# A two-layer decoder trunk: a per-tile router, and eight attention heads placed among the last input projections

## The chip, the cores and the metric

The kernel runs on one core of one Trainium2 chip. The metric is the device time of one execution in microseconds (us). TensorE is called PE here (its weight loads PEld), VectorE DVE, ScalarE ACT, GpSimd POOL; SP issues most of the DMA transfers.

## What is computed

Two layers over 256 tokens of width 1024. Layer 0 is a gated MLP mixer and a dense SwiGLU; the change doesn't touch it. Layer 1 is forgetting attention (16 heads of 64) and an expert SwiGLU, top 2 of 8. Each half of a layer ends in a residual sum and a layer norm, and each layer in a gated per-layer embedding. The part that matters here:

```
def fox_mixer(x, w_in, b_f, w_out):
    q, k, v, f = jnp.split(x @ w_in, [width, 2 * width, 3 * width], axis=-1)
    log_f = jax.nn.log_sigmoid((f + b_f).astype(jnp.float32))
    c = jnp.cumsum(log_f, axis=1).transpose(0, 2, 1)
    for blk in range(s // FOX_BLOCK):
        logits = jnp.einsum("bhtd,bhsd->bhts", q[:, :, q0:q1], k[:, :, :q1])
        logits = logits + c[:, :, q0:q1, None] - c[:, :, None, :q1]
        probs = jax.nn.softmax(jnp.where(mask, logits, -jnp.inf), axis=-1)
        outs.append(jnp.einsum("bhts,bhsd->bhtd", probs, v[:, :, :q1]))
    return o @ w_out

def moe_swiglu(x, w_router, w_gate, w_up, w_down):
    top_vals, top_idx = lax.top_k((x @ w_router), TOP_K)
    weights = jax.nn.softmax(top_vals, axis=-1)
    for e in range(N_EXPERTS):
        out = out + combine[..., e:e + 1] * swiglu(x, w_gate[e], w_up[e], w_down[e])
```

## The kernel before

Everything is written out by hand: each engine has its own program, and semaphores tie them together. No scheduler reorders anything, so an engine that waits holds all that stands behind it in its program. The 256 tokens are two tiles of 128 (T = 2). Weights come in granules of 1 MB (`raw`, 6 slots). ACT rounds each granule to a high part (L604), DVE computes the low part (L921), both into `split` (3 slots), and PE makes three products for each true one (`mm3`, L1478 is the helper that issues every product): high by high, high by low, low by high. `hth` and `htl` hold the high and low parts of the transposed activations.

**Attention.** Six projections of 512 columns (N_FIN = 6, two granules each, 48 products) make q, k and v in PSUM banks 0 to 3 in turn; ACT copies each to `q_nat`, `k_nat` or `v_nat` (L779, L781; semaphore `fin_copied`). The running sums c of the log forget gates are put as two extra columns beside q and k. Then a loop of 19 steps runs the 16 heads as a pipeline. At step s PE transposes q and k of head s (L1806), makes the logits of head s-1 (`qk_t`), transposes the probabilities of head s-2 (L1827) and multiplies the transposed probabilities of head s-3 with v. DVE takes the maxima (L1255), copies the transposed probabilities out of PSUM (L1262), inverts the row sums and scales the result by them (L1269). ACT copies q and k (L795) and makes the exponentials (L802). After the loop `o_nat` is transposed by PE in 16 pieces, split into high and low part by ACT and DVE (L619, L936), and the output projection (four granules, `fox_w_out`) begins. It ends in the norm that makes h of layer 1 (L1009 to L969).

**Router.** PE multiplies h with `w_router` for both tiles (`small`, products with `wrh` and `wrl`), ACT copies the logits (L762), PE turns them (L1773), and DVE ranks them: best and second best (L1304), ties broken by `prio` (L1315 to L1320), membership (`member_b`). PE counts ranks with triangular matrices, DVE makes `slots` and the selection matrices `every` (L1297). PE then gathers each expert's tokens by products of `every` with `xh` and `xl`, the high and low part of h: ACT makes `xh` (L817), POOL makes `xl` (L557). 64 products give 16 banks of gathered tokens, which ACT and DVE copy to `xt`.

**Experts.** 56 blocks (8 experts of 7) of gate, up and down products stream 336 granules through a `ring` of 14 slots. SP loads a slot again when PE has used it, 14 granules ahead; the last two slots of the ring wait for the end of the gather. The outputs of the first seven experts go to the table `expert_rows` in DRAM and are fetched by token at the end; this holds before and after the change.

Around the attention loop PE waits for the copies and for the constants' columns:

```
        pe.wait_ge(fin_copied, T * N_FIN)
        pe.wait_ge(qk_ready, 4 * T)
        for s in range(H + 3):
```

Of the kernel before, what the change touches and what calls it, by code (L numbers as in the profile page):

```python
# [34 lines left out]
def build_trunk(nc, x, p, ln_g, ln_b, gm_w_in, gm_b_in, gm_ln_g, gm_ln_b, gm_w_s, gm_b_s, gm_w_out,  # L35
# [79 lines left out]
    o_nat, nxt = at("o_nat", [P, T, D], F32, par_a)  # L115
# [51 lines left out]
    key = route("key", [P, T])  # L167
# [56 lines left out]
    prob, nxt = at("prob", [P, 2, 3 * P], F32, nxt)  # L224
    prob_t, nxt = at("prob_t", [P, 2, 3 * P], F32, nxt)
    nmax = at("nmax", [P, 2, T], F32, nxt)[0]
    rsum = at("rsum", [P, 2, T], F32, nxt + 32)[0]
    rinv = at("rinv", [P, 2, T], F32, nxt + 64)[0]
# [69 lines left out]
    at_on = sem("at_on")  # L298
# [44 lines left out]
    def flat(t):  # L343
        return t.rearrange("p (c t) n -> p c (t n)", c=2)

# [21 lines left out]
    def _(sp):  # L367
# [57 lines left out]
        for nb in range(N_FIN):  # L425
            for half in range(2):
                load(cols(fox_w_in[0], nb * W, half))
# [50 lines left out]
    def _(pool):  # L478
# [25 lines left out]
        seq(pool.iota(iota_i[:, :], pattern=[[1, P]], base=0, channel_multiplier=0))  # L504
# [69 lines left out]
        pool.wait_ge(rows_ready, 1)  # L574
# [14 lines left out]
    def _(act):  # L589
# [136 lines left out]
        def projected(g, pp, banks):  # L726

            for i in range(2 * T):
# [30 lines left out]
        def small_out(times, bank, n):  # L759

            act.wait_ge(small_full, times)
            nc.scalar.copy(small_t[0:n, :], ps[bank][0:n, 0:S]).then_inc(small_copied, 1)  # L762
# [6 lines left out]
        for i in range(N_FIN):  # L769
            round_hi(G_FIN + 2 * i + 2)  # L770
            round_hi(G_FIN + 2 * i + 3)
            act.wait_ge(s0["used"], G_FIN + 2 * i + 2)
            what, half = i // 2, i % 2
            for m in range(T):
                bank = ps[(i + 1) % 2 * 2 + m]
# [6 lines left out]
                ins.then_inc(fin_copied, 1)  # L782
            if i == 0:
                small_out(1, 5, H)
# [3 lines left out]
            if i == 2:  # L788
                act.wait_ge(f_abs, 2)
                nc.scalar.activation(a_f[:, :, :], a_f[:, :, :], ACT.Ln).then_inc(f_log, 1)  # L790

        for s in range(H + 1):
            if s < H:
                act.wait_ge(at_qk, s + 1)
                nc.scalar.copy(qk_t[0:FA, s % 2, :], ps[6 + s % 2][0:FA, :]).then_inc(at_qkc, 1)  # L795
# [1206 lines left out]
```

## Time and profile before

| | |
|---|---|
| median of 3 runs | 1538.35 us (1537.21 to 1541.26) |
| the profiled execution | 1538.6 us, its span 1536.8 us |
| PE busy | 97% of the span |
| DVE, ACT, POOL busy | 45%, 21%, 3% |
| mean granted TensorE clock | 0.985 |
| chain that ended last | PE 93%, DVE 5% |

By time of the span: layer 0 until about 446 us, the six projections until 515 us, the attention loop and the transposes of its output until 559 us, the output projection until 582 us, norm, router and gather until 618 us, the experts until about 1497 us, then the last scatter, norm and embedding gate. Times below are us from the start of the span. A row of the timeline gives start, duration, engine, line, operation, output<-inputs, shapes and count; what stands in brackets is the idle time of the engine before it and what ended that. In the shape of a product, 128*32 is the stationary tile (rows*columns) and 128x256 what streams past it. Durations of products overlap, so the price of one is the distance from its start to the next start.

### The profile page before, as it was taken

The numbers are of one execution on the slowest core, as the hardware profiler recorded it, in microseconds if no ns is written. First come the engines' busy times: TensorE is split into PE (matmuls) and PEld (weight loads), VectorE is DVE, ScalarE is ACT, GpSimd is POOL, SyncE is SP. The second block draws the span as 40 slices with busy tenths as digits, with TensorE's granted clock in tenths as the row PEclk, the third lists the DMA queues.
The fourth block names the chain that finished last, engine by engine and source line by source line (L and its number), as shares of the span: only waits on it lengthen the run. The fifth ranks groups of instructions, "written<-read, shape, count | busy, mean of one in ns | idle before, by whom it ended". The sixth has DMA issues, their size and how long they took to land.

```text
span 1536.8 us, 33522 instructions
## 1 busy us (share of the span) xinstructions
PE 1483.4 (97%) x15041; PEld 1040.4 (68%) x15041; DVE 699.1 (45%) x1559; ACT 326.3 (21%) x461; POOL 46.5 (3%) x52
## 2 busy tenths in 40 slices
PE   7999899999899997999999999999999999999987
PEld 6888788888688886667666555555555555556665
DVE  5785665555864558332333323232323232323356
ACT  4543443433445543000000000000000000000022
POOL 2010100000100001000000000000000000000020
PEclk9999999999999998999999999999999999999998
DMA  9866455555355315899999999999999999999960
GB/s 371 301 235 211 136 172 214 188 191 191 123 179 173 109 56 192 331 393 409 408 410 406 405 409 411 409 409 406 410 405 408 402 410 404 410 407 411 403 246 28
DMA packets 196094, 468.47 MB, mean 305 GB/s; under 512 B 7740, under 2 KB 8432, under 8 KB 195440
## 3 DMA queue, kind: packets, MB, share of 16 engines
q1 hardware_dynamic: 191392, 450.92, 77.0%
q0 software_dynamic: 2992, 12.70, 2.2%
q10 hardware_dynamic: 1568, 2.75, 0.5%
q8 instruction: 115, 1.88, 0.4%
q14 instruction: 27, 0.22, 0.0%
HBM read 462.53 MB, written 3.81 MB: 303 GB/s over the span
## 4 chain that ended last, share of the span: by engine, by line
PE 93%; DVE 5%; ACT 1%; DMA 1%; issue 0%; DVEq 0%; ACTq 0%
PE ps L1478 90%; PE ps L1495 1%; DVE acc L964 1%; DVE htl L936 1%; DMA ws_raw<-in_gm_w_s_dram 0%; DVE stats L973 0%; PE ps L1806 0%; PE ps L1827 0%; PE ps L1698 0%; DVE h L969 0%; ACT hth L619 0%; DVE split L921 0%; ACT split L604 0%; DVE m_bt L1419 0%; ACT split L647 0%
## 5 line engine op out<-in xcount | busy, mean ns | idle before, releaser
L1478 PE MATMUL ps<-ring,xt 128*32 128x256 f32 (+1 forms) x8064 | 625.9, 451 | 1.1 <-DVE m_hb L1411 1.1
L1478 PEld LDWEIGHTS ps<-ring,xt 128*32 128x32 f32 x8064 | 360.5, 109 | 226.5 <-DVE m_hb L1411 1.6
L1478 PE MATMUL ps<-split,hth 128*128 128x512 f32 x1216 | 384.5, 398 | 8.7 <-DVE htl L936 4.5
L1478 PE MATMUL ps<-ring,m_bt 128*32 128x256 f32 (+1 forms) x4032 | 335.8, 451 | 0.6 <-DVE m_bt L1419 0.6
L1407 DVE TENSOR_TENSOR m_hb<-ps,m_sg 128x256 f32<-128x256 f32 x56 | 23.8, 425 | 573.1 <-ACT m_sg L863 562.7
L1478 PEld LDWEIGHTS ps<-split,hth 128*128 128x128 f32 x1216 | 230.9, 192 | 57.5 <-DVE htl L936 7.8
L1478 PEld LDWEIGHTS ps<-ring,m_bt 128*32 128x32 f32 x4032 | 183.3, 109 | 112.8 <-DVE m_bt L1419 1.0
L1419 DVE STREAM_TRANSPOSE m_bt<-m_hb 32x96 f32<-32x96 f32 x896 | 241.4, 269 | 13.1
L1478 PE MATMUL ps<-split,htl 128*128 128x512 f32 x608 | 240.0, 395 | 0.0
L863 ACT ACTIVATE m_sg<-ps 128x256 f32<-128x256 f32 x56 | 21.5, 383 | 791.7 <-PE ps L1478 791.7
L921 DVE TENSOR_TENSOR split<-raw,split 128x2048 fp32r<-128x2048 f32 x50 | 114.0, 2291 | 83.1 <-ACT split L604 83.0
L1478 PEld LDWEIGHTS ps<-split,htl 128*128 128x128 f32 x608 | 116.5, 192 | 25.1
L604 ACT CAST split<-raw 128x2048 fp32r<-128x2048 f32 x54 | 102.3, 1908 | 57.7 <-PE ps L1478 57.7
L926 DVE TENSOR_TENSOR split<-raw,split 128x2048 fp32r<-128x2048 f32 x36 | 82.0, 2291 | 34.5 <-ACT split L610 34.5
L610 ACT CAST split<-raw 128x2048 fp32r<-128x2048 f32 x36 | 68.5, 1920 | 90.9 <-PE ps L1478 90.9
L1478 PE MATMUL ps<-split,bth 128*128 128x512 f32 x224 | 69.2, 390 | 1.8 <-DVE btl L936 1.6
L1478 PEld LDWEIGHTS ps<-split,bth 128*128 128x128 f32 x224 | 41.9, 188 | 11.1 <-DVE btl L936 1.8
L1478 PE MATMUL ps<-split,btl 128*128 128x512 f32 x112 | 43.6, 389 | 0.0
L936 DVE TENSOR_TENSOR htl<-ps,hth 128x512 fp32r<-128x512 f32 x36 | 23.7, 688 | 21.8 <-ACT hth L619 21.7
L619 ACT CAST hth<-ps 128x512 fp32r<-128x512 f32 x36 | 20.3, 587 | 60.1 <-PE ps L1495 59.8
L1495 PE MATMUL ps<-ident,h 128*128 128x128 f32 x96 | 16.9, 318 | 16.7 <-DVE h L969 12.7
L1121 DVE TENSOR_TENSOR acc<-acc,ps 128x512 f32<-128x512 f32 x28 | 19.2, 686 | 28.0 <-PE ps L1478 28.0
(228 smaller groups left out, 658.3 us busy)
## 6 DMA issues: line engine op xcount, KB each, us to landing
ring<-in_moe_w_gate_dram SPq DMA_DIRECT2D x112, 1024.0 KB, 12.1
ring<-in_moe_w_up_dram SPq DMA_DIRECT2D x112, 1024.0 KB, 13.2
ring<-in_moe_w_down_dram SPq DMA_DIRECT2D x112, 1024.0 KB, 12.2
raw<-in_gm_w_in_dram SPq DMA_DIRECT2D x14, 1024.0 KB, 13.3
raw<-in_ffn_w_gate_dram SPq DMA_DIRECT2D x14, 1024.0 KB, 5.0
raw<-in_ffn_w_up_dram SPq DMA_DIRECT2D x14, 1024.0 KB, 5.9
raw<-in_ffn_w_down_dram SPq DMA_DIRECT2D x14, 1024.0 KB, 4.9
raw<-in_fox_w_in_dram SPq DMA_DIRECT2D x12, 1024.0 KB, 5.2
```

Of the source, the lines that this page charges most:

```text
L604: nc.scalar.copy(split[:, ss, 0], raw[:, slot]).then_inc(st["hi"], 1)
L610: nc.scalar.copy(split[:, gs % SPL, 0], raw[:, gs % RAW]).then_inc(s0["hi"], 1)
L619: nc.scalar.copy(dst, bank[:, 0:n].rearrange("p (c t) -> p c t", t=P)).then_inc(st["tp_hi"], 1)
L863: nc.scalar.activation(m_sg[:, 0:2 * P].rearrange("p (q n) -> p q n", n=P), ps[0][:, :].rearrange("p (q x) -> p q x", x=2 * P)[:, :, 0:P], ...
L921: nc.vector.tensor_tensor(split[:, ss, 1], raw[:, slot], split[:, ss, 0].bitcast(F32), ALU.subtract)\
L926: nc.vector.tensor_tensor(split[:, gs % SPL, 1], raw[:, gs % RAW], split[:, gs % SPL, 0].bitcast(F32), ALU.subtract).then_inc(s0["lo"], 1)
L936: nc.vector.tensor_tensor(dst, bank[:, 0:n].rearrange("p (c t) -> p c t", t=P), hi.bitcast(F32), ALU.subtract).then_inc(st["tp_lo"], 1)
L1121: nc.vector.tensor_tensor(part, part, ps[bank][:, :], ALU.add).then_inc(part_added, 1)
L1407: nc.vector.tensor_tensor(m_hb[:, 0:2 * P].rearrange("p (q n) -> p q n", n=P), ps[0][:, :].rearrange("p (q x) -> p q x", x=2 * P)[:, :, P: ...
L1419: last = nc.vector.transpose(m_bt[s * G3:(s + 1) * G3, b % 2, q, :, :], blocks[:, :, s, :])
L1478: return nc.tensor.matmul(o, a, b, start=start, stop=stop)
L1495: last = nc.tensor.transpose(ps[6 + n % 2][:, c * P:(c + 1) * P], src, ident[:, :])
```

## The change

1. **Heads among projections.** The projections come in another order of columns (`FIN_COLS`: first halves of q, k and v, then the second halves). The last three all use banks 0 and 1. The steps of attention 0 to 10 are placed among their products (`STEP_AFTER`), after every 12 products or so; steps 11 to 16 follow; steps 17 to 19 stand among the products of the output projection.
2. **Another step.** The probabilities are scaled before they are transposed (DVE, `at_norm`), one step later, and there are three `prob` buffers but only one PSUM bank for the transposes. v is now the stationary tile of 64 columns, for two heads at a time, so that the result comes out transposed in bank 5: ACT and DVE split it (`at_ohi`, `at_olo`) straight into the inputs of the output projection. `o_nat` and its 16 transposes are gone.
3. **Router.** Each tile has its own logits, turn and ranking; tile 0's products are placed ahead of tile 1's transposes. Ranking is shorter. Slots start at one instead of zero.
4. **Gather.** DVE makes `xl` (POOL no longer does), between the two halves of `every`; PE starts with the products of `xh`. The weights and the row numbers are computed after the gather's copies.

The diff, cut to its core:

```diff
-    GX_BANK = (0, 1, 4, 5, 6, 7, 0, 1, 4, 5, 6, 7, 4, 5, 6, 7)
+    GX_BANK = (6, 7, 4, 5, 0, 1, 6, 7, 4, 5, 6, 7, 4, 5, 6, 7)
+    FIN_COLS = (0, 2, 4, 1, 3, 5)
+    STEP_AFTER = {(3, 1): 0, (3, 2): 1, (3, 3): 2, (4, 0): 3, (4, 1): 4, (4, 2): 5, (4, 3): 6,
+                  (5, 0): 7, (5, 1): 8, (5, 2): 9, (5, 3): 10}
...
 POOL
-        for m in range(T):
-            pool.wait_ge(xh_ready, m + 1)
-            pool.tensor_tensor(xl[:, m, :], h[:, m, :], xh[:, m, :].bitcast(F32), ALU.subtract)\
-                .then_inc(xl_ready, 1)
+        pool.wait_ge(rows_ready, 1)
...
 ACT, after the third projection
+        for i in (4, 5):
+            round_hi(G_FIN + 2 * i + 2)
+            attend(4 * i - 13)
+            attend(4 * i - 12)
+            round_hi(G_FIN + 2 * i + 3)
+            attend(4 * i - 11)
+            fin_out(i)
+            attend(4 * i - 10)
+        for s in range(11, H + 1):
+            attend(s)
...
 DVE
+        def attend(s):
+            if 0 <= s - 2 < H:
+                hd = s - 2
+                dve.wait_ge(at_exp, T * (hd + 1))
+                seq(nc.vector.reciprocal(rinv[:, hd % 3, :], rsum[:, hd % 3, :]))
+                for m, (a, b) in enumerate(((0, P), (P, 3 * P))):
+                    part = prob[:, hd % 3, a:b]
+                    ins = nc.vector.tensor_scalar(part, part, rinv[:, hd % 3, m:m + 1], None, ALU.mult)
+                ins.then_inc(at_norm, 1)
+            if s >= 6 and s % 2 == 0:
+                p = (s - 6) // 2
+                dve.wait_ge(at_ohi, p + 1)
+                nc.vector.tensor_tensor(o_chunk(p, 1), ps[5][:, 0:S], o_chunk(p, 0).bitcast(F32), ALU.subtract)\
+                    .then_inc(at_olo, 1)
+            if 0 <= s - 1 < H:
...                (the two maxima of head s-1)
+            if 0 <= s - 3 < H:
...                (waits at_pt, copies prob_t)
...
+            seq(nc.vector.tensor_copy(lg[:, m, :], ps[3 + 2 * m][:, m * NE:(m + 1) * NE]))
             seq(nc.vector.max(top8[:, m, :], lg[:, m, :]))
+            seq(nc.vector.tensor_scalar(eqk[:, m, :], lg[:, m, :], top8[:, m, 0:1], 16.0, ALU.is_equal, ALU.mult))
...
+            seq(nc.vector.max(two8[:, m, :], eqk[:, m, :]))
+            nc.vector.tensor_scalar(member_b[:, m, :], eqk[:, m, :], two8[:, m, 1:2], None, ALU.is_ge)\
+                .then_inc(mem_ready, 1)
...
+        select_every(first_experts, (0,))
+        rest_x(0)
+        select_every(first_experts, (1,))
...
+        gathered(0)
+        route_weights()
+        rows_to_gather()
         dve.wait_ge(acc_init, 2 * T)
...
 PE
+            if s >= 5 and s % 2:
+                p = (s - 5) // 2
+                pe.wait_ge(at_ptc, 2 * p + 2)
...
+                for m in range(T):
+                    for b in range(2):
+                        hd = 2 * p + b
+                        last = mm(ps[5][b * DH:(b + 1) * DH, m * P:S], v_nat[:, m, hd * DH:(hd + 1) * DH],
+                                  prob_t[:, b, m * S:m * S + (T - m) * P], m == 0, m == T - 1)
...
+        for i in range(N_FIN):
+            if i == 2 or i == 3:
+                pe.wait_ge(fin_copied, T * (i - 1))
+            elif i > 3:
+                pe.wait_ge(fin_copied, T * i)
...
+        small(2, NE, wrh, wrl, fresh, (0,))
         turn_tile(1)
-        small(2, NE, wrh, wrl, fresh)
-        small_turn(3, NE, 2).then_inc(lg_full, 1)
+        small_turn(3, NE, 2, (0,)).then_inc(lg_full, 1)
+        pe.wait_ge(proj_copied, 3 * T)
+        small(4, NE, wrh, wrl, fresh, (1,))
+        small_turn(5, NE, 3, (1,)).then_inc(lg_full, 1)
```

PE at the end of the last projection, in the program before: the projection's last products, then step 0 of the attention loop, which waits for the copies of all projections (counting from the start of the program, lines are those of the file before).

```order
L1478 MATMUL ps<-split,hth 128x512 x2
L1478 MATMUL ps<-split,htl 128x512
L1806 MATMUL ps<-ident,q_nat 66x128 [waits qk_ready,fin_copied]
L1806 MATMUL ps<-ident,q_nat 66x128
```

In the changed program a step stands between products of the fifth projection (this is step 5, with the first pair of heads; `prob_t,v_nat` is the product with v):

```order
L1543 MATMUL ps<-split,htl 128x512
L1860 MATMUL ps<-ident,q_nat 66x128 [waits at_qkc]
L1860 MATMUL ps<-ident,q_nat 66x128
L1860 MATMUL ps<-ident,k_nat 66x128 x2
L1543 MATMUL ps<-qk_t 128x128 [waits at_exp,at_qkc]
L1543 MATMUL ps<-mask,ident_b 128x128
L1543 MATMUL ps<-qk_t 128x256
L1543 MATMUL ps<-mask,ident_b 128x128
L1543 MATMUL ps<-prob_t,v_nat 64x256 [waits at_ptc]
L1543 MATMUL ps<-prob_t,v_nat 64x256
L1543 MATMUL ps<-prob_t,v_nat 64x128 x2
L1896 MATMUL ps<-ident,prob 128x128 [waits at_ptc,at_norm]
```

What moved: steps 0 to 10 now have projection products between them, and the wait for all copies is split into smaller ones.

DVE in an even step of the changed program (here step 6): the scaling of head 4 waits for its exponentials and stands ahead of the maxima of head 5.

```order
L1264 RECIPROCAL rinv<-rsum 128x2 [waits at_exp]
L1267 TENSOR_SCALAR prob<-prob,rinv 128x128 [waits dve_step]
L1267 TENSOR_SCALAR prob<-prob,rinv 128x256
L1272 TENSOR_TENSOR otl<-ps,oth 128x256 [waits at_ohi]
L1278 TENSOR_REDUCE nmax<-ps 128x1 [waits at_log]
L1278 TENSOR_REDUCE nmax<-ps 128x1
L1285 COPY prob_t<-ps 128x384 [waits at_o,at_pt]
```

What moved: before, the maxima stood first in a step and waited for PE alone.

DVE in the router of the changed program, from the second tile's membership to the gather's copies:

```order
L1371 TENSOR_SCALAR member_b<-eqk,two_102 128x8 [waits dve_step]
L1378 TENSOR_TENSOR member<-eqk,two_102 128x16
L1379 TENSOR_TENSOR gap<-top_100 128x2 [waits dve_step]
L1383 TENSOR_TENSOR slots<-member,ps 128x2x8 [waits rank_full]
L1350 TENSOR_TENSOR every<-iota,slots 128x384 [waits dve_step]
L1350 TENSOR_TENSOR every<-iota,slots 128x384
L1357 TENSOR_TENSOR xl<-h,xh 128x1024 [waits xh_ready] x2
L1350 TENSOR_TENSOR every<-iota,slots 128x384 x2
L1433 COPY xt<-ps 128x384 [waits gx_full] x8
```

What moved: `xl` came here from POOL, and 26 small operations that stood ahead of the copies now stand behind them.

## Rows read from the trace of the kernel before

**Rows 1.** Experts: busy us by engine, then clock, DMA share, GB/s.

```profile
619.00:1500.00 881.00, 874.06 (x12105) 534.61 (x12093) 292.71 (x1025) 47.11 (x139) 13.85 (x6) 1.00 1.02 398
```

**Rows 2.** Timeline of PE: gate and up products of two expert blocks.

```profile
1251.73 9.88 PE L1478 MATMUL ps<-ring,xt 128*32 128x256 f32 x135
...
1267.27 9.88 PE L1478 MATMUL ps<-ring,xt 128*32 128x256 f32 x135
```

**Rows 3.** Timeline of ACT: copies after the third and last projection.

```profile
481.92 1.08 ACT L779 COPY k_nat<-ps 128x512 f32<-128x512 f32 x2 [3.47 <-PE ps L1478]
...
515.25 1.07 ACT L781 COPY v_nat<-ps 128x512 f32<-128x512 f32 x2 [3.48 <-PE ps L1478]
```

**Rows 4.** Timeline of PE: transposes of the output, output projection, its end.

```profile
554.76 1.97 PE L1495 MATMUL ps<-ident,o_nat 128*128 128x128 f32 x8 [0.38 <-DVE o_nat L1269]
...
558.89 1.20 PE L1478 MATMUL ps<-split,hth 128*128 128x512 f32 x2
...
582.49 1.32 PE L1495 MATMUL ps<-ident,h 128*128 128x128 f32 x8
```

**Rows 5.** Timeline of PE: start of attention, one step of it.

```profile
516.38 0.41 PE L1806 MATMUL ps<-ident,q_nat 128*66 128x128 f32 x2 [1.17 <-ACT v_nat L781]
...
520.82 0.38 PE L1806 MATMUL ps<-ident,q_nat 128*66 128x128 f32 x2
...
521.53 0.65 PE L1478 MATMUL ps<-qk_t 66*128 66x256 f32 x2
...
522.08 0.50 PE L1827 MATMUL ps<-ident,prob 128*128 128x128 f32 x3
522.41 0.78 PE L1478 MATMUL ps<-v_nat,prob_t 128*128 128x64 f32 x6
523.03 0.38 PE L1806 MATMUL ps<-ident,q_nat 128*66 128x128 f32 x2
```

**Rows 6.** Timeline of PE: router and gather.

```profile
590.75 1.32 PE L1495 MATMUL ps<-ident,h 128*128 128x128 f32 x8 [1.49 <-DVE h L969]
...
595.40 0.28 PE L1773 MATMUL ps<-ident,small_t 8*128 8x8 f32 x2 [0.45 <-ACT small_t L762]
602.77 0.22 PE L1478 MATMUL ps<-member_b,upper_b 128*128 128x8 bf16 x2 [7.09 <-DVE member_b L1324]
...
605.36 0.66 PE L1478 MATMUL ps<-every,xh 128*128 128x384 f32 x1 [2.29 <-DVE every L1297]
...
618.39 3.88 PE L1478 MATMUL ps<-ring,xt 128*32 128x512 f32 x50
```

**Rows 7.** Timeline of DVE: router.

```profile
596.42 2.32 DVE L1315 TENSOR_TENSOR eqk<-lg,top 128x16 f32<-128x16 f32 x1
598.78 2.28 DVE L1318 TENSOR_TENSOR eqk<-eqk,prio 128x16 f32<-128x16 f32 x1
...
604.18 1.96 DVE L1297 TENSOR_TENSOR every<-iota,slots 128x384 fp32r<-128x384 f32 x4
...
611.14 1.48 DVE L1367 COPY xt<-ps 128x384 f32<-128x384 f32 x3
```

**Rows 8.** Timeline of POOL: the low part of h.

```profile
596.38 4.64 POOL L557 TENSOR_TENSOR xl<-h,xh 128x1024 fp32r<-128x1024 f32 x2 [177.42 <-ACT xh L817]
```

**Rows 9.** Timeline of PE: two products of the gather, later.

```profile
614.13 0.33 PE L1478 MATMUL ps<-every,xh 128*128 128x384 f32 x1
614.31 0.33 PE L1478 MATMUL ps<-every,xl 128*128 128x384 f32 x1
```

**Rows 10.** Timeline of ACT: first and last piece of a step's exponentials.

```profile
523.00 0.37 ACT L802 ACTIVATE prob<-ps,nmax 128x128 f32<-128x128 f32 x1 [0.88 <-DVE nmax L1255]
...
523.72 0.20 ACT L802 ACTIVATION_READ_ACCUMULATOR prob<-ps,nmax 128x1 f32 x1
```

**Rows 11.** Timeline of DVE: the maxima of one attention step.

```profile
522.35 0.62 DVE L1255 TENSOR_REDUCE nmax<-ps 128x1 f32<-128x128 f32 x2 [0.70 <-PE ps L1478]
```

**Rows 12.** The same view as Rows 1, 3 us of the gather.

```profile
606.00:609.00 3.00, 3.00 (x11) 3.00 (x10) 2.56 (x15) 0.48 (x1) 0.00 (x0) 0.50 0.00 0
```

More of the change, by code:

```diff
@@ L724, in _, with projected @@
         round_hi(g + G_EXP - 1)
[L726 to L728 removed]
+        def projected(g, pp, banks, of=range(2 * T)):
+            for i in of:
                 act.wait_ge(s0["used"], g + 1)
@@ L1289, in select, with select_every @@
             ins.then_inc(sel_ready, 1)
-        def select_every(at_e):
-            for half in range(2):
+        def select_every(at_e, halves=range(2)):
+            for half in halves:
                 for m in range(T):
@@ L1754, in _, with small @@
         n_fin = nt[0] - T
-        def small(bank, n, wsh, wsl, fresh):
-            for m in range(T):
+        def small(bank, n, wsh, wsl, fresh, tiles=range(T)):
+            for m in tiles:
                 tok = slice(m * P, (m + 1) * P)
@@ new lines, in attend @@
+                mm(bank[:, 2 * P:3 * P], ident_b[:, :], mask[:, :], False, True).then_inc(at_log, 1)
+            if s >= 5 and s % 2:
+                p = (s - 5) // 2
+                pe.wait_ge(at_ptc, 2 * p + 2)
+                if p >= 1:
+                    pe.wait_ge(at_olo, p)
+                if p == H // 4:
+                    pe.wait_ge(fin_copied, T * N_FIN)
+                for m in range(T):
+                    for b in range(2):
+                        hd = 2 * p + b
+                        last = mm(ps[5][b * DH:(b + 1) * DH, m * P:S], v_nat[:, m, hd * DH:(hd + 1) * DH],
+                                  prob_t[:, b, m * S:m * S + (T - m) * P], m == 0, m == T - 1)
+                last.then_inc(at_o, 1)
@@ new lines, in out_granule @@
+        def out_granule(g, m):
+            tok = slice(m * P, (m + 1) * P)
+            for kk in range(2):
+                k = 2 * (g - G_FOUT) + kk
+                for half in range(2):
+                    last = mm3(ps[2 * m + half][:, :], oth[:, k, tok], otl[:, k, tok], g % SPL, 2 * kk + half,
+                               k == 0, False)
+            if m == T - 1:
+                last.then_inc(s0["used"], 1)
+        for i in range(N_FIN):
[3 more added lines that the diff above has]
+                pe.wait_ge(fin_copied, T * i)
+            if i < 3:
+                cols_granules(G_FIN + 2 * i, [(i + 1) % 2 * 2, (i + 1) % 2 * 2 + 1], fresh=n_fin if i == 0 else None,
+                              between={0: lambda: turn_half(1),
+                                       1: lambda: small_turn(4, H, 1).then_inc(f_full, 1)}.get(i))
+            else:
+                fin_block(i)
+            if i == 0:
+                pe.wait_ge(small_split, 4)
+                small(5, H, wfh, wfl, None)
+            if i == 2:
+                pe.wait_ge(f_logf, 1)
+                pe.wait_ge(const_ready, 1)
+                prefix(5, H, z_f, upper, ones).then_inc(c_full, 1)
```

383 lines of the change are left out of this document (203 added, 180 removed).

## The prediction

> **What bounds the kernel now.** I read the page first: PE is busy in 97% of the span, and the chain that ended last lies on PE for 93%. So only what PE does, or waits for, can move the time. The experts' stage is the longest: PE is busy 874 of 881 us in it, at the full clock [rows 1], and a block follows the last at 15.54 us (1267.27 - 1251.73) [rows 2]; 56 such blocks are 870 us. The reader is to see that this stage is a fixed length that begins when the gather ends. The change leaves its products alone. The DMA share there is as full as PE (398 GB/s), which comes back among the rivals. Everything that the change can give must come before the first expert product, at 618.39.
>
> Next I read the timeline of PE from the third projection to there, in two stretches.
>
> *Attention, 481.9 to 582.5 us, 100.6 us.* Three projections take 33.3 (from 481.92 to 515.25, the copies that follow them) [rows 3]. From 515.3 to 558.89, 43.6 us, stand the heads and the output's transposes, and from there to 582.49 the output projection, 23.6 us [rows 4]. Within the heads a step takes 2.21 us (523.03 - 520.82), back to back on PE: 1.26 for transposes of q and k and the logits, 0.33 for the transposes of the probabilities, 0.62 for the product with v [rows 5]. So PE's own work bounds the heads, 16 x 2.21 = 35.4, and the other 8.2 us are filling, emptying, the wait of 1.17 for v [rows 5] and the output's transposes with their split.
>
> *Router, 590.75 to 618.39 us.* PE waits 7.09 us for membership and 2.29 for the selection matrices; the gather takes 13.0 (605.36 to 618.39) [rows 6]. The wait of 7.09 is odd in its make-up. DVE runs two operations of 16 columns in 2.32 and 2.28 us [rows 7], while 26 operations of like size between the end of `every` (606.14) and 611.14 take 0.19 each [rows 7]. POOL's two subtractions on `xl` lie exactly beside them, 596.38 to 601.02 [rows 8]. DVE was held by POOL.
>
> **The change, part by part.**
>
> *Heads on PE.* Interleaving saves no product, so I count PE's work. Transposes and logits stay: 16 x (1.26 + 0.33) = 25.4 us. The product with v now has v as a stationary tile of 64 columns, and two heads write different halves of a bank: two products over 256 columns and two over 128. One product over 256 with its mask takes 0.55 (522.08 - 521.53) [rows 5]. One after the other the four are at most 2 x 0.55 + 2 x 0.28 = 1.65 us; two at a time, 0.83. Before, two heads cost 1.24. The experts' products of 32 columns show 135 issues of 256 columns in 9.88 us [rows 2], 0.07 each, where an issue over 256 columns of a full tile takes some 0.27 [rows 5]: narrow tiles do run side by side, four at a time. So I take the low end, with a little for switching, 0.9: 8 x 0.9 = 7.2. Heads: 32.6 us.
>
> Where the gather's full tile gives way to the experts' narrow one, the trace names no idle time ahead of the block [rows 6], and the gather's products start 0.17 apart [rows 9]. The Trainium skill (TensorEngine Tiling, Key Properties) says that changing the tiling mode drains the engine, which speaks against this step: sixteen changes. It gives no price. If each cost 0.1 us, half of them in stretches where PE waits anyway, the sum would be 0.8 us longer; the 0.9 above stays as it is.
>
> *Output's transposes.* Sixteen transposes and their splits, from 554.76 to 558.89, leave the path [rows 4]. The splits become one ACT copy and one DVE subtraction for each pair, beside PE.
>
> *Output projection.* Two issues take 1.20 us at 558.89 [rows 4], where the clock was low; without the gap before it the clock should not fall. At the projections' rate, 33.3/6 for a granule, four are 22.2; with the embedding's transposes, and a share of the 33.3 that is not granules, 22.5.
>
> *New waits.* (a) The last three projections share banks 0 and 1, so the sixth waits for the copies of the fifth. ACT has step 5's exponentials and the first output copy ahead of these copies: I find them some 1.0 us later than PE. For the fifth projection ACT is in time. (b) At the sixth's end ACT copies v (1.07 us [rows 3]) and then q and k of head 10: 0.5 us for step 11. (c) DVE now scales head s-2 ahead of the maxima of head s-1, and the scaling waits for the exponentials, which wait for the maxima. That is a loop through two engines, once a head: exponentials 0.92 (523.00 to 523.92) [rows 10], maxima 0.62 [rows 11], scaling about 0.7, the subtraction of the low part every second step 0.17, hand-overs 0.1. Sum 2.5 us, against 2.0 of PE's work. For the scaling no row exists. A reciprocal is one small operation, 0.19; the products of 128 and 256 columns cost at least 0.19 each and at most the 0.49 of 384 columns in `every` [rows 7]: 0.57 to 1.17, and I take 0.7, as one source and fewer columns are nearer the low end. Steps 0 to 10 are covered, since 12 projection products (2.8 us) lie between two steps. Steps 11 to 16 are not: 6 x 2.5 = 15.0 where PE has 12.2, so 2.8 us of waiting. If that cover didn't hold, ten more steps would lose 0.5 each.
>
> Sum: 33.3 + 32.6 + 22.5 + 1.0 + 0.5 + 2.8 = 92.7 against 100.6: **7.9 us less**. The bounds: loop at 2.3 or at 3.0, -1.2 and +3.0; pairs one after the other, about five on the path x 0.75 = +3.8; no waits, -4.3.
>
> The skill bears on the scaling alone. The one-source operations here read and write SBUF in fp32. The Trainium skill (VectorE: DVE Perf Modes, the perf-mode tier table) lets such a `tensor_scalar` run at twice the rate of a two-source operation; taken so, the scaling would be near 0.6 and the loop 2.4, and the stretch 0.6 us shorter.
>
> *Router.* POOL's hold goes: 4.6 us become 2 x 0.19, a gain of 4.2. Of the 14 operations between logits and membership, 7 are left behind the second tile's logits, tile 0's being done while that tile is still split: 7 x 0.19 = 1.3. Tile 0's 24 small products move into the 1.49 us in which PE waits for h [rows 6]; the second tile's are then held by its own split, so I count 0.5 (0 to 1.5). Slots take one operation, not four, and the count moves behind: 4 x 0.19 = 0.8 of the 2.29. Sum 6.8. What is added: `xl` on DVE, two operations of 1024 columns, at least 1.0 each and at most POOL's 2.3 [rows 8]; I take 1.2. PE meanwhile has twelve products of `xh`, 0.17 each at the full clock (614.31 - 614.13) [rows 9], 2.1 us, twice that at half. Of the 2.4 at most 0.3 shows; likely 0.1. At POOL's price it would be 2.5. The gather keeps its length: 64 x 0.175 = 11.2 at the full clock, 13.0 measured, since the clock was at half (0.50) until about 609 [rows 12], behind 7 us of idleness. There are still some 4 idle us ahead of it, so I leave that loss in. **6.7 us less.**
>
> *Behind the gather.* 29 small DVE operations (5.5 us) and an exponential on ACT now stand between the copies and the first block's hidden product. The first gate and up products cover them, 9.88 us [rows 2]. If the cover were gone, 7 us would come on top once. SP's order is as before, and POOL's next work (a memset, the table's zero row) waits for the row numbers and is needed only at the end.
>
> Total 7.9 + 6.7 = 14.6. The profiled execution took 1538.6, 0.25 over the median, so the sum gives 1524.0 against it: **1524.0 us** forecast.
>
> **The rivals.**
> - *Better cover.* The clock stays full through the router (1.8 us, 13.0 - 11.2), or the loop and the waits (a) and (b) don't show (up to 4.3). Together 1518. For it: only 4 us of idleness. Against: most of those 4 are in one piece. Chance 0.12 for under 1519.5.
> - *Pairs one after the other, or a longer loop.* +3.8 and +3.0: 1528 to 1531. For it: no product of 64 columns of this kind is in the trace. Chance 0.19 for 1528 to 1533.9.
> - *The gain is given back.* If the loads bound the experts, starting sooner would bring nothing, and the time would be 1538. For it: DMA share 1.02. Against: blocks at PE's pace of 15.54 and 7 us of idleness in 881 [rows 1, 2]; and the loads start sooner too. Chance 0.06 of within 0.3%.
> - *Slower: half clock.* In steps 11 to 16 PE idles a fifth of the time in small pieces. Should the clock fall to 1.2 GHz there and stay there over the output projection, 12.2 + 22.5 = 34.7 us of work double, less the 2.8 of waiting that this hides: +32, or 1556. It decides once more than 14.6 us of PE's work run at half. Against: a steady step before has much the same work. Chance 0.05.
>
> **How the numbers follow.** My forecast (1519.5 to 1528) has 0.58. 1516 to 1533 leaves out the last two rivals and the ends of the others, about 0.2. A measurement can tell about 0.3% (4.6 us) from no change: faster 0.89, same 0.06, slower 0.05.
>
> **What would show it.** In the profile after: no idle time of 7 us ahead of the rank products, and no DVE operation of 16 columns over 1 us; pairs of products with v at about 0.9 us; steps 11 to 16 about 2.5 us apart, with PE waiting for q, k or the copies; output projection at the full clock; the experts still 15.54 a block. The forecast is wrong if the experts' stage grows, if the clock falls in the uncovered steps, or if the router's wait moves to `xl`.

## The result, and the profile after

The changed kernel takes 1521.97 us (median; 1521.48 to 1523.24) against 1538.91 us (1537.21 to 1541.26) for the kernel before on the same chip. The ratio is 0.989, with a 95% interval of 0.9877 to 0.9903: 17 us faster, 2.0 us better than the forecast of 1524.0 and inside its range. In part that closeness is luck: terms that were off both ways partly cancel, as the section on the prediction shows. The profiled execution took 1521.48, its span 1519.7.

PE is as full as it was. First the line of the page for the engines, then the experts' stage: busy us of PE, PEld, DVE, ACT and POOL, the granted clock, the DMA share and GB/s; then two successive blocks' gate and up products on PE's timeline.

```profile
PE 1476.3 (97%) x14993; PEld 1029.4 (68%) x14993; DVE 701.8 (46%) x1581; ACT 327.4 (22%) x466; POOL 42.0 (3%) x50
```

```profile
602.00:1483.00 881.00, 874.31 (x12101) 535.10 (x12093) 297.46 (x1054) 50.55 (x143) 14.73 (x8) 1.00 1.02 398
```

```profile
1219.14 9.88 PE L1543 MATMUL ps<-ring,xt 128*32 128x256 f32 x135
...
1234.68 9.88 PE L1543 MATMUL ps<-ring,xt 128*32 128x256 f32 x135
```

They answer to [rows 1, 2]: 874 of 881 us busy, 398 GB/s, 1234.68 - 1219.14 = 15.54 us a block, as before. The gain lies ahead of the experts. Between the copies behind the third projection (481.64 after; 481.92 in [rows 3]) and the first expert product, the two stretches of the prediction are:

| stretch | before | after | gain | predicted |
|---|---|---|---|---|
| attention, to the transposes of h | 100.6 | 91.0 | 9.5 | 7.9 |
| router and gather | 35.9 | 28.7 | 7.2 | 6.7 |

With the 0.3 us by which the copies came earlier these make the 17.1 us between the spans.

**Attention.** PE's timeline in the changed kernel, from a step among the projections, through the uncovered steps 11 to 16, to the output projection and the transposes of h. Columns: start, us, then line, operation, output and inputs, shape, count, and in brackets the idle time with its releaser.

```profile
508.90 0.22 PE L1543 MATMUL ps<-mask,ident_b 128*128 128x128 bf16 x1
509.05 0.87 PE L1543 MATMUL ps<-prob_t,v_nat 128*64 128x256 f32 x8
509.85 0.55 PE L1896 MATMUL ps<-ident,prob 128*128 128x128 f32 x3
...
533.50 0.22 PE L1543 MATMUL ps<-mask,ident_b 128*128 128x128 bf16 x1
533.56 0.50 PE L1896 MATMUL ps<-ident,prob 128*128 128x128 f32 x3
533.90 0.38 PE L1860 MATMUL ps<-ident,q_nat 128*66 128x128 f32 x2
...
535.25 0.87 PE L1543 MATMUL ps<-prob_t,v_nat 128*64 128x256 f32 x8
...
539.76 0.87 PE L1543 MATMUL ps<-prob_t,v_nat 128*64 128x256 f32 x8 [0.28 <-DVE prob_t L1285]
...
542.76 0.38 PE L1860 MATMUL ps<-ident,k_nat 128*66 128x128 f32 x2
543.24 0.49 PE L1543 MATMUL ps<-qk_t 66*128 66x128 f32 x2
...
544.62 0.87 PE L1543 MATMUL ps<-prob_t,v_nat 128*64 128x256 f32 x8 [0.28 <-DVE prob_t L1285]
...
547.25 0.71 PE L1543 MATMUL ps<-split,oth 128*128 128x512 f32 x2
...
572.67 1.32 PE L1560 MATMUL ps<-ident,h 128*128 128x128 f32 x8 [0.21 <-DVE h L1006]
```

A pair of products with v lasts 0.80 us (509.05 to 509.85), with 0.15 ahead of it where a transpose comes only 0.06 behind the same product with the mask (533.50, 533.56). Steps 11 to 16 last 13.35 us (533.90 to 547.25); the reader is to see how little of it is waiting. The brackets say 0.28 twice; by the distances between starts these two pairs come 0.36 later than one that needn't wait (0.51 behind the mask product in place of 0.15). Between the transposes of k and the logits lie 0.48 us once (542.76 to 543.24), where 0.22 is usual. Leaving the narrow tile has a price too. The last issue of a pair, over 128 columns, and the first transpose behind it:

```profile
509.65 0.27 PE L1543 MATMUL ps<-prob_t,v_nat 128*64 128x128 f32 x1
509.85 0.33 PE L1896 MATMUL ps<-ident,prob 128*128 128x128 f32 x1
```

They start 0.20 apart, where issues over 128 columns within the pair follow each other at 0.11 in each half. This is part of the pair's 0.80.

What sets the pitch in these steps is on ACT and DVE: first the exponentials of three successive heads on ACT, then DVE from the first of them on.

```profile
539.27 0.37 ACT L803 ACTIVATE prob<-ps,nmax 128x128 f32<-128x128 f32 x1 [0.94 <-DVE nmax L1278]
...
541.54 0.37 ACT L803 ACTIVATE prob<-ps,nmax 128x128 f32<-128x128 f32 x1 [0.88 <-DVE nmax L1278]
...
544.13 0.37 ACT L803 ACTIVATE prob<-ps,nmax 128x128 f32<-128x128 f32 x1 [0.94 <-DVE nmax L1278]
```

```profile
540.22 0.17 DVE L1264 RECIPROCAL rinv<-rsum 128x2 f32<-128x2 f32 x1 [0.52 <-ACT prob L803]
540.42 0.55 DVE L1267 TENSOR_SCALAR prob<-prob,rinv 128x128 f32<-128x128 f32 x2
540.89 0.61 DVE L1278 TENSOR_REDUCE nmax<-ps 128x1 f32<-128x128 f32 x2
...
542.69 0.55 DVE L1267 TENSOR_SCALAR prob<-prob,rinv 128x128 f32<-128x128 f32 x2
543.15 0.42 DVE L1272 TENSOR_TENSOR htl<-ps,hth 128x256 fp32r<-128x256 f32 x1
543.48 0.61 DVE L1278 TENSOR_REDUCE nmax<-ps 128x1 f32<-128x128 f32 x2
```

The loop of the prediction is there: exponentials from 539.27, reciprocal at 540.22, scaling at 540.42, maxima at 540.89, the next exponentials at 541.54. It takes 2.27 us, and 2.59 where the low part of the output stands between scaling and maxima (543.15 to 543.48): 2.43 a head.

**Router.** PE, from the rank products to the first expert product; then DVE, in the second tile's ranking and at `xl`; then the clock in the gather's first part.

```profile
586.92 0.20 PE L1543 MATMUL ps<-member_b,upper_b 128*128 128x8 bf16 x2 [1.66 <-DVE member_b L1371]
...
588.62 3.78 PE L1543 MATMUL ps<-every,xh 128*128 128x384 f32 x12 [1.42 <-DVE every L1350]
592.23 2.24 PE L1543 MATMUL ps<-every,xl 128*128 128x384 f32 x12
...
601.34 1.93 PE L1543 MATMUL ps<-ring,xt 128*32 128x512 f32 x23
```

```profile
585.97 0.23 DVE L1367 SCALAR_TENSOR_TENSOR eqk<-lg,top,eqk 128x8 f32<-128x8 f32 x1
586.23 0.17 DVE L1369 TENSOR_TENSOR eqk<-eqk,prio 128x8 f32<-128x8 f32 x1
...
588.39 2.35 DVE L1357 TENSOR_TENSOR xl<-h,xh 128x1024 fp32r<-128x1024 f32 x2
```

```profile
588.00:592.00 4.00, 3.38 (x11) 3.41 (x12) 3.68 (x6) 0.00 (x0) 0.00 (x0) 0.57 0.47 180
```

The waits of 7.09 and 2.29 us [rows 6] are 1.66 and 1.42. No small DVE operation is longer than 0.23, where two took 2.32 and 2.28 [rows 7]. `xl` takes 2.35 on DVE for both tiles, and PE doesn't wait for it. The gather takes 12.72 us (588.62 to 601.34); the clock is at half from 588.4 to 591.8 (0.57 in the mean of the row). Before it was at half from 598.9 to 609.1, of which 3.8 us lay in the gather [rows 12], so that the gather itself lost nearly as much then.

### The profile page after: what moved, and what is told of

Read it like the earlier page. It is cut to its first block, busy times and chain, and to the rows that moved or that the text cites. A ratio compares the mean times of both kernels' runs of the same rounds, so it can differ in the third digit from the quotient of the medians.

```text
span 1519.7 us, 33431 instructions
## 1 busy us (share of the span) xinstructions
PE 1476.3 (97%) x14993; PEld 1029.4 (68%) x14993; DVE 701.8 (46%) x1581; ACT 327.4 (22%) x466; POOL 42.0 (3%) x50
## 4 chain that ended last, share of the span: by engine, by line
PE 92%; DVE 5%; ACT 1%; DMA 1%; issue 1%; DVEq 0%; ACTq 0%
PE ps L1543 90%; PE ps L1560 1%; DVE acc L1001 1%; DVE stats L1010 0%; DMA ws_raw<-in_gm_w_s_dram 0%; DVE htl L973 0%; ACT split L613 0%; PE ps L1763 0%; DVE h L1006 0%; DVE split L958 0%; PE ps L1860 0%; PE ps L1896 0%; ACT hth L628 0%; DVE m_bt L1485 0%; ACT prob L803 0%
## 5 line engine op out<-in xcount | busy, mean ns | idle before, releaser
L1543 PE MATMUL ps<-split,hth 128*128 128x512 f32 x1184 | 374.3, 398 | 8.7 <-DVE htl L973 4.5
L1543 PEld LDWEIGHTS ps<-split,hth 128*128 128x128 f32 x1184 | 223.6, 191 | 56.0 <-DVE htl L973 7.8
L1543 PE MATMUL ps<-split,htl 128*128 128x512 f32 x592 | 233.5, 394 | 0.0
L1543 PEld LDWEIGHTS ps<-split,htl 128*128 128x128 f32 x592 | 113.1, 191 | 24.3
```

The costliest lines, as they stand in the source:

```text
L1543: return nc.tensor.matmul(o, a, b, start=start, stop=stop)
```

## The experiments

Where a kernel's time is one single run, I compare stretches of its trace instead; the last section says why. The attention stretch is then measured from `z_f,upper`, the small table products behind the third projection (481.44 in the changed kernel), to the transposes of h (572.67): 91.23 us, and to the start of the output projection (547.25): 65.81.

**The parts alone.** First the router's part alone, then attention's part alone; each takes the other part's text from the kernel before. One piece of each, against the changed kernel (the loop of PE in the first, `xl` in the second):

```
-        for s in range(11, H + 1):
-            attend(s)
...
+        for s in range(H + 3):
```

```
-                rest_x(dve.snap(r * T))
...
+            pool.tensor_tensor(xl[:, m, :], h[:, m, :], xh[:, m, :].bitcast(F32), ALU.subtract)\
+                .then_inc(xl_ready, 1)
```

> The kernel before with the router and gather part of the change alone (per-tile ranking, low part of h on DVE, weights after the gather). Theory (the two parts lie one behind the other on PE's path and add up): the stretch from the first transposes of h to the first expert product shortens from 35.9 to about 28.7 us, and the kernel takes 1538.9 - 7.2 = 1531.7 us. Rival (the router's stretch got shorter only because the loads and the clock stood otherwise after the new attention): less than 4 us gained, above 1535 us.

> The kernel before with the attention part of the change alone (heads among the last projections, the new step, no transposes of the output). Theory: the stretch up to the end of the output projection shortens by 9.8 us as in the whole change, the router keeps its 35.9 us with DVE held twice for 2.3 us; about 1529.1 us. Rival (the parts help each other): the two single gains together are under 14 us.

Measured: the router alone 1532.94 us (1530.51 to 1533.76), ratio 0.9952 (0.9935 to 0.9968) to 1539.74 of before. Attention alone 1530.2 (1528.65 to 1530.54), ratio 0.9935 (0.9918 to 0.9952). The gains are 6.8 and 9.5, together 16.3, against 17; each of the two has an interval of some 2.5 us either way, so the stretches say more. In the trace of the first, transposes of h to the first expert product is 28.77 us (583.75 to 612.52), as in the changed kernel; in that of the second it is 35.71 (573.96 to 609.67), with the old waits of 7.09 and 2.29. Each part shortens its own stretch and leaves the other's as it was.

**POOL's hold.** `xl` goes back to POOL, all else stays:

```
+            pool.tensor_tensor(xl[:, m, :], h[:, m, :], xh[:, m, :].bitcast(F32), ALU.subtract)\
+                .then_inc(xl_ready, 1)
...
-        rest_x(0)
```

> The changed kernel with the low part of h made by POOL again, the rest as it is. Theory (POOL's subtractions hold DVE): they start when the high part is ready, about 586 us, in the midst of the second tile's ranking; a DVE operation of 8 or 16 columns there takes about 2.3 us in place of 0.2, once or twice, so that the first expert product comes 2 to 4.5 us later than at 601.3. Rival (the long operations of before had another cause, the wide operands or the shape of the operation): no DVE operation of the ranking over 0.3 us, first expert product within 0.7 us of 601.3, since POOL's 4.6 us would end about when the twelve products with the high part do.

Measured: 1526.66 us. DVE and POOL during the second tile's ranking, and PE at the rank products:

```profile
585.64 2.41 DVE L1371 SCALAR_TENSOR_TENSOR eqk<-lg,top,eqk 128x8 f32<-128x8 f32 x1
585.68 4.64 POOL L570 TENSOR_TENSOR xl<-h,xh 128x1024 fp32r<-128x1024 f32 x2 [167.21 <-ACT xh L858]
...
588.08 2.26 DVE L1373 TENSOR_TENSOR eqk<-eqk,prio 128x8 f32<-128x8 f32 x1
...
590.88 0.22 PE L1546 MATMUL ps<-member_b,upper_b 128*128 128x8 bf16 x2 [5.95 <-DVE member_b L1375]
```

Two operations of 8 columns take 2.41 and 2.26 us instead of 0.23 and 0.17 while POOL's two subtractions run, 4.27 in all, and PE's wait grows from 1.66 to 5.95. The stretch from the transposes of h to the first expert product is 34.11 us (572.34 to 606.45) against 28.67, 5.4 more and not the 2 to 4.5 that I expected. Of these, 4.3 are the hold and 1.1 the gather, 13.86 against 12.72, as the clock was at half from 588.0 to 598.2 here and from 588.4 to 591.8 in the changed kernel. That this 1.1 comes from the hold isn't shown: two kernels below without a hold have gathers of 14.00 and 14.10. The Trainium skill (GPSIMD Engine Reference, Specifications) says that GpSimd's SBUF interfaces are shared with VectorE and contend with its instructions that have two SBUF inputs. The trace agrees: both held operations have two.

**The maxima first.** In the changed kernel DVE scales head s-2 ahead of the maxima of head s-1. Here it is the other way round:

```
         def attend(s):
+            if 0 <= s - 1 < H:
...
             if 0 <= s - 2 < H:
...
-            if 0 <= s - 1 < H:
```

> The changed kernel with the maxima of head s-1 ahead of the scaling of head s-2 in DVE's step. Theory (steps 11 to 16 are bound by the loop exponentials, scaling, maxima): the loop is cut, two steps take PE's 4.1 to 4.3 us in place of 4.86, and the output projection starts 0.7 to 1.4 us sooner than at 547.25. Rival (they are bound by DVE's or ACT's work, or by the single bank of the transposes): steps stay at 4.86 for two.

Measured: 1524.41 us, of which 1.2 over the changed kernel's trace lie ahead of the table products and 1.3 in the gather, so that the attention stretch has to decide. The output projection starts 66.39 us behind the table products, not 65.81, and the transposes of h 91.80, not 91.23. So taking the scaling out of the loop brought nothing. PE waits more, and elsewhere:

```profile
537.08 0.87 PE L1543 MATMUL ps<-prob_t,v_nat 128*64 128x256 f32 x8 [0.57 <-DVE prob_t L1285]
...
541.86 0.87 PE L1543 MATMUL ps<-prob_t,v_nat 128*64 128x256 f32 x8 [0.57 <-DVE prob_t L1285]
```

Two steps last 4.78 us (541.86 - 537.08), against 4.86 in the changed kernel (544.62 - 539.76). But the pair now waits 0.57 for `prob_t`, already at the first uncovered pair: DVE copies the transposed probabilities behind maxima, scaling and low part, and in these two steps it waits itself, 0.71 for PE's logits and 0.25 for PE's transposes. I read this as a second loop, through PE, that has taken the first one's place; no run tests that reading. The order moved the wait and hardly changed the length of a step.

The gather of this run shows something else. Its router has the same program and the same waits, and yet it took 14.00 us (590.37 to 604.37). Its first products, and the clock from 592 to 596:

```profile
590.37 4.18 PE L1543 MATMUL ps<-every,xh 128*128 128x384 f32 x12 [1.42 <-DVE every L1350]
```

```profile
592.00:596.00 4.00, 4.00 (x14) 4.00 (x14) 1.56 (x4) 0.48 (x1) 0.00 (x0) 0.50 0.00 1
```

The clock was at half from 589.4 to 596.3. Among the seven traces with this router and without extra products or POOL's subtractions, five have gathers of 12.60 to 12.84 us (the changed kernel's 12.72 among them) and two of 14.00 and 14.10. What makes the difference stays open.

**The low part behind the maxima.** Only the subtraction, 0.33 us in every second step, goes out of the loop:

```
+            if 0 <= s - 1 < H:
...
             if s >= 6 and s % 2 == 0:
...
-            if 0 <= s - 1 < H:
```

> The changed kernel with one edit on VectorE: in the even steps the subtraction of the low part stands behind the maxima, not ahead of them. In the changed kernel the exponentials of the uncovered steps are 2.27 and 2.59 us apart in turn. Theory (the loop of exponentials, scaling and maxima sets the pitch there, and the subtraction lies in it only in even steps): both become 2.27, PE's work of 2.11 a head nearly fills it, and the output projection starts 0.6 to 0.8 us earlier (65.0 to 65.2 us behind the last small table products, against 65.81); time 0.7 below the changed kernel. Rival (VectorE's whole work in a step sets the pitch, so its order does not matter, as with the maxima first, which gave nothing): 65.7 to 65.9, no change.

Measured: 1523.25 us. Exponentials of four heads on ACT:

```profile
536.74 0.37 ACT L803 ACTIVATE prob<-ps,nmax 128x128 f32<-128x128 f32 x1 [0.37 <-DVE nmax L1273]
...
539.00 0.37 ACT L803 ACTIVATE prob<-ps,nmax 128x128 f32<-128x128 f32 x1 [0.89 <-DVE nmax L1273]
...
541.26 0.37 ACT L803 ACTIVATE prob<-ps,nmax 128x128 f32<-128x128 f32 x1 [0.61 <-DVE nmax L1273]
...
543.52 0.37 ACT L803 ACTIVATE prob<-ps,nmax 128x128 f32<-128x128 f32 x1 [0.88 <-DVE nmax L1273]
```

They are 2.26 us apart each time. The output projection starts 65.26 us behind the table products (548.97 - 483.71), 0.55 earlier, and so do the transposes of h (90.68 us behind them, not 91.23). That is what the loop, and not DVE's whole work, demands; it is somewhat under the 0.6 to 0.8 expected. The single time doesn't show it, because this run's opening was 2.3 us later.

**Without the cover.** All 17 steps stand behind the sixth projection, nothing else changes:

```
-    STEP_AFTER = {(3, 1): 0, (3, 2): 1, (3, 3): 2, (4, 0): 3, (4, 1): 4, (4, 2): 5, (4, 3): 6,
-                  (5, 0): 7, (5, 1): 8, (5, 2): 9, (5, 3): 10}
+    STEP_AFTER = {}
...
-        for s in range(11, H + 1):
+        for s in range(H + 1):
```

> The changed kernel with all steps of attention after the last projection, the projections in two pairs of banks in turn as before; the new step, its transposed output and the steps among the output projection stay. Theory (the loop through ACT and DVE costs 2.43 us a head where nothing covers it, PE's work is 2.0): the output projection starts 5 to 7 us later than 547.25, the whole takes 1527 to 1529 us, still below the attention of before since the output's transposes are gone. Rival (placing heads among projections brings nothing, as PE does the same products anyway; all the gain is from the transposes that went): within 1.5 us of 1522.

Measured: 1528.3 us (1528.08 to 1529.88), ratio 0.9925 (0.9908 to 0.9942) to before: 6.3 above the changed kernel, or 5.4 by the two ratios. The output projection starts 71.91 us behind the table products (553.96 - 482.05), 6.1 later. PE's waits from 515 to 554 (us in total, how often, the longest):

```profile
PE ps L1524 <- DVE prob_t L1274: 1.7, 6, 0.3
PE ps L1841 <- ACT v_nat L788: 1.2, 1, 1.2
PE ps L1524 <- ACT qk_t L795: 1.1, 3, 0.4
PE ps L1877 <- DVE prob_t L1274: 0.5, 2, 0.3
```

So of attention's 9.5 us, the cover gives two thirds, part of it by removing the wait for v that stood ahead of the first head (1.17 in [rows 5]) and the filling behind it. The remaining third, about 3.4, stays without the cover. I put it down to the cheaper product with v and the output's transposes that are gone, less the waits of the new loop; no run takes these apart.

**Side by side or not.** Two kernels on the pair of products with v. The first issues head by head (256 columns, 128, 256, 128) where the changed kernel issues both products of 256 columns first. The second writes both heads to the same half of the bank; the upper 64 rows of each output piece are then not computed.

```
-                for m in range(T):
-                    for b in range(2):
+                for b in range(2):
+                    for m in range(T):
```

```
-                        last = mm(ps[5][b * DH:(b + 1) * DH, m * P:S], v_nat[:, m, hd * DH:(hd + 1) * DH],
+                        last = mm(ps[5][0:DH, b * S + m * P:b * S + S], v_nat[:, m, hd * DH:(hd + 1) * DH],
```

> The changed kernel with the four products of a pair with v in the order head, then token tile, so that neighbours write the same half of the bank but for one place. Theory (products of 64 columns in different halves run side by side, and the order gives them the chance): a pair takes 1.2 to 1.5 us in place of 0.8 (the middle two may still overlap), the last projection ends 1 to 2 us later and the whole takes 1523.5 to 1526. Rival (the engine runs them one after the other in either order, and 0.8 is simply their price): no change.

> The changed kernel, but the products with v of both heads of a pair write the same 64 partitions (partitions 0 to 63) of the bank, head by head; the upper 64 rows of the attention output are then not computed, and the times are to be read so. In the changed kernel a pair takes 0.80 us in either order. Theory (the two heads' narrow products run side by side in different halves of TensorE, and the order does not matter because each half takes its own in turn): in one half they must run one after the other, the pair takes about 1.3 to 1.45 us. Then the three pairs between projections (steps 5, 7, 9) and the one in the output projection add 0.5 to 0.6 each, and the uncovered ones partly: stretch from the last small table products to the transposes of h 93 to 95 us against 91.2, time about 1524.5. Rival (they never ran side by side, a narrow product is simply cheap): the pair stays at 0.80 and the stretch at 91.2, time 1522.

Measured: head by head 1521.15 us, and the pair lasts 0.81 (508.71 to 509.52), as before: my expectation fell. Same half 1526.4 us, and the pair lasts 1.44. First PE's instructions by shape, head by head, in the window from 508.70 to 509.15 (count, then busy us and mean ns); then the timeline of the same half.

```profile
L1543 PE MATMUL ps<-prob_t,v_nat 128*64 128x256 f32 x4 | 0.7, 404 | 0.0
```

```profile
508.88 1.51 PE L1543 MATMUL ps<-prob_t,v_nat 128*64 128x256 f32 x8
510.32 0.55 PE L1896 MATMUL ps<-ident,prob 128*128 128x128 f32 x3
```

The second kernel shows that the heads do run side by side: without it a pair costs 0.64 us more, the transposes of h come 95.06 us behind the table products (576.32 - 481.26), 3.8 later. Eight pairs would be 5.1; the waits of 0.28 ahead of the uncovered pairs are gone in this run, which accounts for part of the missing 1.3. The time lies 1.9 above the expected 1524.5, of which 1.4 is this run's gather (14.10, see above). The first shows why the order is nothing: each product is two issues, and by 509.15 all four over 256 columns have started and none over 128, though the issues over 128 columns of head 0 stand between them in the program. They don't hold the other half's products. The Trainium skill (TensorE: Matmul & The Clock Gate, Part 3, The mechanism) says that matmuls start and end strictly in program order. This trace shows another order than the kernel's text for products in different halves, and the measurement decides. Whether the chip changed the order, or the instructions already came to it in this one, no run here tells.

**The gather's clock.** 26 bf16 products ahead of the rank products and 22 ahead of the gather, which nothing reads, keep PE at work during the two waits:

```
+        for _ in range(26):
+            mm(ps[6][:, 0:P], ident_b[:, :], upper_b[:, :], True, True)
         pe.wait_ge(mem_ready, T)
...
+        for _ in range(22):
+            mm(ps[6][:, 0:P], ident_b[:, :], upper_b[:, :], True, True)
         gather(0, 1, T)
```

> The changed kernel with 26 and 22 idle products of 128 columns (bf16, into a bank that the gather overwrites) on PE ahead of its waits for membership and for the selection matrices; they add work and no result. Theory (the clock at half in the first products of the gather comes from PE's idleness before it): the granted clock stays at full, the first twelve products take 2.1 us in place of 3.6, and the first expert product comes 1 to 1.5 us sooner relative to the start of the ranking. Rival (the 3.6 us are waits or the fall has another cause): the half clock and the 3.6 us stay.

Measured: 1520.85 us. PE's twelve products of `xh`, and the clock beside them:

```profile
589.34 2.33 PE L1543 MATMUL ps<-every,xh 128*128 128x384 f32 x12 [0.17 <-DVE every L1350]
```

```profile
588.00:592.00 4.00, 3.83 (x36) 3.51 (x34) 3.96 (x7) 0.55 (x2) 0.00 (x0) 1.00 0.61 231
```

The gather starts as before, 15.96 us behind the transposes of h (15.95), and its first twelve products take 2.33 instead of 3.78. It is 1.3 us shorter (28.67 to 27.36 for the stretch), and the clock is granted full. So half the clock, behind waits of 1.66 and 1.42 us with little between, is what the gather still lost: with the extra products it takes 11.40 us, without them 12.60 to 12.84 or, twice, 14.00 and 14.10.

**Both together.** The extra products with the maxima first, and with the low part behind:

> The changed kernel with both the maxima first and the idle products. Theory: the two gains add, 1.7 to 2.9 us below the changed kernel's 1522, 1519.1 to 1520.3 us. Rival (what is gained ahead of the experts is lost in the first block, as DVE's 29 small operations behind the gather then end later than the first gate and up products): no faster than 1522.

> The low part behind the maxima, and the 26 and 22 extra bf16 products ahead of the rank products and of the gather, whose results nothing reads. Theory: the two gains add, 0.7 (uncovered steps) and 1.3 (gather at the full clock), so about 1520.0 us against 1522.0 of the changed kernel. Rival: only the extra products count, 1520.7. Should either cost more than it gives: 1522 or above.

Measured: with the maxima first 1522.27 us (1521.1 to 1523.29), ratio 0.9882 (0.9865 to 0.9898); no gain beyond the changed kernel's 0.989. Its attention stretch is 0.6 longer (91.82), its gather 1.3 shorter. With the low part behind 1520.76 (1520.24 to 1521.6), ratio 0.9882 (0.9866 to 0.9899). In the trace of the latter, from the table products to the first expert product, 118.00 us (482.09 to 600.09) stand against 119.90: 1.9 less, 0.6 of it in the uncovered steps and 1.3 in the gather. The medians differ by 1.2, and the two intervals overlap, so that it is faster is shown by the stretches and not yet by the times.

## Why the prediction was right, step by step

- *The bound.* The experts' stage is a fixed length that begins when the gather ends: 15.54 us a block before and after, and no gain was given back. That rival (0.06) is out.
- *POOL's hold, ranking and small products, 6.0 us.* Measured from the transposes of h to the rank products: 20.28 before (582.49 to 602.77), 14.25 after, so 6.03. The hold itself, 4.2 in the sum, is 4.3 in the run that brings it back.
- *Slots, 0.8.* From the rank products to the gather 2.59 before, 1.70 after: 0.9.
- *`xl` on DVE, 1.2 us for each of two, nearly hidden.* Both took 2.35, against the 2.4 of the sum. They were hidden, since PE's twelve products of `xh` took 3.6 at the half clock. At the full clock, in the run with the extra products, `xl` ends at 591.46 and its first product starts at 591.52, some 0.1 us behind the twelve products of `xh`, which is the 0.1 of the sum.
- *The gather, unchanged.* It became 0.3 us shorter, where I had it 0.1 longer. I kept the whole loss to the clock although the waits ahead shrank from 9.4 to 3.1 us, and that was nearly right: 3.8 us of the gather ran at half before, 3.2 after. It is also luck, since two other traces with the same router and the same waits have 1.3 us more.
- *A pair at 0.9 us.* 0.80, and 0.95 with what lies ahead of it. Side by side is shown. The Trainium skill's (TensorEngine Tiling, Key Properties) drain at a change of mode fits the prices here, about 0.1 us going in (0.15 against 0.06) and about 0.1 coming out (0.20 against 0.11), the size that was supposed; both are small beside the 0.64 that running side by side saves.
- *Waits (a) 1.0 and (b) 0.5.* Neither is there. PE comes to step 6 right behind the fifth projection; its 1.5 us of transposes, logits and probabilities (512.99 to 514.51) hide the copies, which are 1.08 (from 513.19). I had set ACT's lateness against the next projection product and left out the step in between. The same holds for (b).
- *The loop, 2.5 us a head, 2.8 of waiting.* The pitch was right (2.43; scaling with reciprocal 0.67 for 0.7), its count was not. I charged all six steps. Step 11 and the pair at 535.25 still lived on the lead that DVE and ACT had from the covered steps, and the last head's transposes and the last two pairs stand among the output projection's products, where nobody waits for them. Of 13.35 us about 1.4 is waiting, by the distances between starts: 0.36 ahead of each of two pairs, 0.34 ahead of the last transposes (0.40 in place of 0.06), and for q and k 0.26 ahead of the logits and 0.11 within them.
- *PE's own work.* Here I was about 1.3 too low: a head's share without waits is 2.08 (535.25 to 539.76 are 4.51, less 0.36, halved), not 2.04, which is 0.6 over sixteen heads; the rest, about 0.7, falls to the output projection. So 2.9 too much waiting and 1.3 too little work make the 1.6 by which attention came out better. The total was closer than its terms.
- *Cover gone, 0.5 a step for ten steps.* 6.1 us in the stretch, not 5: the filling of the pipeline and the wait for v, which I hadn't put into that figure, are covered as well.
- *The slower rival, half clock from step 11 on.* The clock was 1.00 through the attention stretch; the half clock that before fell at the output's transposes (0.57 over 554 to 562) isn't there.

## What to carry to other kernels

When a loop through two other engines is slower than the main engine's work, charge its lag only to the steps that have neither a lead behind them nor other work among them; here the pitch was right and the count was not. Ahead of moving an operation to the front of such a loop, look for the next loop: here taking the scaling out moved the wait, while taking out the one short operation that nobody waited for gave nearly all that it should. Where an engine with nothing else to do shares its way to memory with the one on the path, giving its work to the latter can be the gain itself.

## What the runs showed of the hardware that I had not expected

- Products in one half of TensorE start ahead of ones that stand earlier in the kernel's text and belong to the other half, as shown above, with what put them in this order left open; two heads cost 0.80 us in either order and 1.44 in one half.
- The opening varies from run to run. Of eleven kernels with the same text up to the third projection (the changed one and all but the one with the router's part alone), the table products behind it start anywhere from 481.07 to 483.71 us. The four later than 482.5 have the clock at half around 17 us. The window from 14 to 20 us in the changed kernel, then in the one with the low part behind:

```profile
14.00:20.00 6.00, 4.36 (x19) 3.63 (x20) 5.48 (x9) 6.00 (x9) 2.28 (x3) 1.00 1.05 411
```

```profile
14.00:20.00 6.00, 3.84 (x14) 2.94 (x13) 4.90 (x8) 5.84 (x9) 1.72 (x2) 0.78 1.05 409
```

PE had less to do there (3.84 us against 4.36), and the clock was 0.78 instead of 1.00. What delays it in one run and not in another stays open. With the gather's two lengths, 12.60 to 12.84 and 14.00 to 14.10, it is why a difference of one microsecond was read here from a stretch of attention, and not from one time.
